# Issue order of one score chunk and of the router's steps in the attention stage of a diffusion layer

## What is computed

```python
fx, qx, kx, vx = split_projection(hx @ w_in[l])
qx = axial_rope(heads(qx, N_Q_HEADS, q_norm_g[l]), row, col)    # 12 heads of 64
kx = axial_rope(heads(kx, N_KV_HEADS, k_norm_g[l]), row, col)   # 4 heads of 64
...
s = jnp.einsum('bqkgd,bskd->bkgqs', qi, k_all).astype(jnp.float32) * (HEAD_DIM ** -0.5)
p = jax.nn.softmax(s, axis=-1).astype(v_all.dtype)              # over 1280 keys
o = jnp.einsum('bkgqs,bskd->bqkgd', p, v_all)
...
x = x + g1 * (jnp.concatenate([four_x, attn_x], axis=-1) @ w_out[l])
h = modulate(x, norm_ffn_g[l], sh2, sc2)
aff = jax.nn.softmax(jnp.einsum('bnd,de->bne', h, w_router), axis=-1)   # 16 experts
x = x + g2 * (the 16 experts on the 128 tokens that each of them picks by aff)
return rms_norm(x, final_norm_g)
```

## Time and profile before

| | |
|---|---|
| median of three runs | 2030.63 us (2030.01 to 2036.04) |
| the profiled execution: its own time | 2035.89 us |
| its span, first to last instruction | 2033.3 us |
| busy: TensorE, VectorE, ScalarE, GpSimd | 1856.9 us (91%), 1614.0 (79%), 1303.5 (64%), 290.0 (14%) |
| attention stage | about 266 to 862 us of the span |
| tile steps by the copy L921: 5th, 6th, 7th | 71.85, 71.88, 73.15 us |
| mean granted TensorE clock of the span | 0.964 of full speed |
| slot 1 of the step shown, scores to scores (619.85 to 623.17) | 3.32 us, TensorE without idle |
| TensorE, start to start: wide score chunk, then one item with its values (664.67, 665.23, 665.91) | 0.56 us, 0.68 us |

### The profile page before, as it was taken

How to read it: one execution, slowest core, us unless ns; L and a number is a source line. 1 busy time by engine, 2 the same in 40 slices (tenths; PEclk the granted TensorE clock), 3 DMA queues, 4 the chain that set the end, 5 groups by cost and what they waited for, 6 DMA issues and landing times.

```text
span 2033.3 us, 28027 instructions
## 1 busy us (share of the span) xinstructions
PE 1856.9 (91%) x8691; PEld 1462.4 (72%) x8691; DVE 1614.0 (79%) x2070; ACT 1303.5 (64%) x1921; POOL 290.0 (14%) x294
## 2 busy tenths in 40 slices
PE   6998869899899889719999999999999999999996
PEld 3776647666666666517888888888888888888884
DVE  5777547766766767487989998999899989998996
ACT  4444347666766766416777777777777777777774
POOL 0233221110111111101101100110011001110113
PEclk8999879999999999958999999999999999999998
DMA  8556480210110120039999999999999999999996
GB/s 353 172 151 170 109 228 28 63 41 22 62 44 28 52 62 10 31 120 365 396 394 390 376 377 402 389 381 370 405 386 384 368 404 386 373 384 398 380 379 245
DMA packets 108034, 512.28 MB, mean 252 GB/s; under 512 B 12064, under 2 KB 36040, under 8 KB 57296
## 3 DMA queue, kind: packets, MB, share of 16 engines
q1 hardware_dynamic: 101792, 489.11, 63.7%
q0 software_dynamic: 4752, 17.30, 3.2%
q10 hardware_dynamic: 1440, 5.24, 0.7%
HBM read 481.71 MB, written 27.28 MB: 250 GB/s over the span
## 4 chain that ended last, share of the span: by engine, by line
PE 54%; DVE 2%; DMA 1%; issue 0%; ACT 0%; POOL 0%
PE banks L1599 34%; PE banks L1624 17%; PE banks L1611 1%; PE banks L1580 1%; DVE topi L1458 1%; DVE top L1456 1%; DVE cand L1459 1%; DMA xe<-h_scratch,icol 0%; DVE raw L1554 0%; DMA out<-raw 0%; DVE ysc L1518 0%; DVE ysc L1561 0%; ACT d_hi L1421 0%; POOL out L1381 0%; DVE x_lo L1484 0%
## 5 line engine op out<-in xcount | busy, mean ns | idle before, releaser
L1490 DVE TENSOR_TENSOR w_lo<-raw,w_hi 128x2048 fp32r<-128x2048 f32 x256 | 574.8, 2287 | 67.9 <-ACT w_hi L1399 67.9
L1399 ACT ACTIVATE w_hi<-raw 128x2048 fp32r<-128x2048 f32 x256 | 470.8, 1919 | 10.5 <-DMA raw<-in_w_exp 10.4
L1599 PE MATMUL banks<-w_hi,x_hi 128*128 128x512 f32 x1024 | 406.2, 397 | 1.4 <-DVE x_lo L1484 1.4
L1599 PE MATMUL banks<-w_hi,x_lo 128*128 128x512 f32 x1024 | 400.6, 391 | 0.0
L1599 PE MATMUL banks<-w_lo,x_hi 128*128 128x512 f32 x1024 | 400.1, 391 | 0.0
L1498 DVE TENSOR_TENSOR d_lo<-raw,d_hi 128x1024 fp32r<-128x1024 f32 x256 | 296.2, 1218 | 1.5 <-ACT d_hi L1421 1.4
L1421 ACT ACTIVATE d_hi<-raw 128x1024 fp32r<-128x1024 f32 x256 | 258.1, 1060 | 38.5 <-DMA raw<-in_w_exp 24.7
L1058 DVE TENSOR_TENSOR ptl<-banks,pth 128x384 fp32r<-128x384 f32 x320 | 176.6, 555 | 66.8 <-ACT pth L995 61.5
L995 ACT ACTIVATE pth<-banks 128x384 fp32r<-128x384 f32 x320 | 156.9, 490 | 109.3 <-PE banks L1168 101.1
L1599 PEld LDWEIGHTS banks<-w_hi,x_lo 128*128 128x128 f32 x1024 | 192.9, 188 | 40.7
L1599 PEld LDWEIGHTS banks<-w_hi,x_hi 128*128 128x128 f32 x1024 | 193.2, 189 | 39.7 <-DVE x_lo L1484 1.8
(11 more groups left out here) (213 smaller groups left out, 2768.4 us busy)
## 6 DMA issues: line engine op xcount, KB each, us to landing
raw<-in_w_exp SPq DMA_DIRECT2D x384, 1024.0 KB, 8.0
a_ring<-in_w_mod SPq DMA_DIRECT2D x32, 512.0 KB, 5.0
qt<-q_scratch SPq DMA_DIRECT2D x64, 192.0 KB, 3.6
a_slot<-in_w_mod SPq DMA_DIRECT2D x8, 1024.0 KB, 12.0
a_w_raw<-in_w_in SPq DMA_DIRECT2D x3, 2048.0 KB, 30.2
q_scratch<-a_qst SPq DMA_DIRECT2D x16, 384.0 KB, 3.9
a_xt<-in_x ACTq DMA_DIRECT2D x8, 512.0 KB, 6.1
xr<-in_x SPq DMA_DIRECT2D x8, 512.0 KB, 4.0
```

Of the source, the lines that this page charges most:

```text
L1399: act.activation(w_hi[which][c][:, :], raw[which][c][:, :], ACT.Copy).then_inc(s["hi_done"], 1)
L1490: dve.tensor_tensor(w_lo[which][c][:, :], raw[which][c][:, :], w_hi[which][c][:, :].bitcast(F32), ALU.subtract).then_inc(s["lo_done"], 1)
L1599: i = pe.matmul(psum[:, 2 * (j % 2) + which, :], x_[par][:, k, :], w_, start=(k == 0 and w_ is hi and x_ is x_hi), stop=(k == KD - 1 and x ...
```

## The change

Four edits:

1. **Scores.** TensorE issues chunk 1 of a head at the end of part 1, behind that part's transposes and value products; chunk 2 follows at once at the start of part 2. VectorE reduces chunk 1 behind correction 1.
2. **Logit factor.** The first stage multiplies the key gain once by minus the logit factor. Scores then come out negated and scaled: VectorE takes minima (`mn`, in place of `mx` and `nb`), the small minimum is itself the bias, L1054 goes, and the exponential has scale -1.
3. **The shift of h2** is added on GpSimd in two halves of 512; HT0 waits for the first only, the store for both.
4. **Router chain.** HT0 stays at the end of slot 8 (part 3); HT1 moves from the end of slot 9 to its part 2, ahead of the fourth item; the router's product from the end of slot 10 to its part 0; maximum and negative to part 1 of slot 10; the exponential to part 2 of slot 10; reciprocal and scaling to part 0 of slot 11; the transpose to part 1 and the copy of the affinities to part 2 of slot 11.

```diff
@@ scaled (first stage, VectorE)
                 if n == 0:
                     dve.wait_ge(s["kv_tab"], 32)
+                    link(dve.tensor_scalar(g_qk[:, 1, :], g_qk[:, 1, :], -SCALE, None, ALU.mult))
@@ SP
-                    sp.wait_ge(s["h2b"], t if cur else t + 1)
+                    sp.wait_ge(s["h2b"], 2 * t)
@@ GpSimd
                     if prev and cur and i == 8:
                         pool.wait_ge(s["h2a"], t)
-                        pool.tensor_tensor(h2[:, :], h2[:, :], rows[:, SH2, :], ALU.add).then_inc(s["h2b"], 1)
+                        for c in (slice(0, 512), slice(512, D)):
+                            pool.tensor_tensor(h2[:, c], h2[:, c], rows[:, SH2, c], ALU.add).then_inc(s["h2b"], 1)
+                        pool.wait_ge(s["h2b"], 2 * t)
@@ ScalarE
                             act.activation(pr[(h // 3 % 2) * 3 + h % 3][:, lo:hi], psum[:, (NCH * h + c) % 4, 0:hi - lo], ACT.Exp,
-                                           bias=nb[:, h:h + 1], scale=SCALE, accum_out=den[:, h, c:c + 1]).then_inc(s["exp_done"], 1)
+                                           bias=mn[:, h, 3:4], scale=-1.0, accum_out=den[:, h, c:c + 1]).then_inc(s["exp_done"], 1)
...
+                        if prev and (i, c) == (9, 3):
...
+                        if prev and (i, c) == (10, 2):
+                            act.wait_ge(s["neg_done"], t)
...
+                        if prev and (i, c) == (11, 2):
+                            act.wait_ge(s["misc_mm"], misc(t, use["AF"]) + 1)
...
@@ VectorE
-                        if cur and c < NCH:
+                        if cur and c in (0, 2):
                             lo, hi = CH[c]
                             dve.wait_ge(s["s_done"], NS * t + NCH * i + c + 1)
-                            ins = dve.tensor_reduce(mx[:, i, c:c + 1], psum[:, (NCH * i + c) % 4, 0:hi - lo], AX, ALU.max)
+                            ins = dve.tensor_reduce(mn[:, i, c:c + 1], psum[:, (NCH * i + c) % 4, 0:hi - lo], AX, ALU.min)
                         if cur and c == NCH - 1:
                             chain(ins)
 
-                            chain(dve.tensor_reduce(mx[:, i, 3:4], mx[:, i, 0:3], AX, ALU.max))
-                            dve.tensor_scalar(nb[:, i:i + 1], mx[:, i, 3:4], -SCALE, None, ALU.mult).then_inc(s["nb_done"], 1)
+                            dve.tensor_reduce(mn[:, i, 3:4], mn[:, i, 0:3], AX, ALU.min).then_inc(s["mn_done"], 1)
                         if c < len(its):
...
+                        if cur and c == 1:
+                            lo, hi = CH[c]
+                            dve.wait_ge(s["s_done"], NS * t + NCH * i + c + 1)
+                            ins = dve.tensor_reduce(mn[:, i, c:c + 1], psum[:, (NCH * i + c) % 4, 0:hi - lo], AX, ALU.min)
...
+                        if prev and (i, c) == (10, 1):
+                            dve.wait_ge(s["misc_mm"], misc(t, use["RT"]) + 1)
+                            chain(dve.tensor_reduce(lg[:, 2, 1:2], psum[:, MB, 0:E], AX, ALU.max))
+                            dve.tensor_scalar(st2[:, 3:4], lg[:, 2, 1:2], -1.0, None, ALU.mult).then_inc(s["neg_done"], 1)
+                        if prev and (i, c) == (11, 0):
+                            dve.wait_ge(s["lexp"], t)
+                            chain(dve.reciprocal(lg[:, 2, 2:3], lg[:, 2, 0:1]))
+                            dve.tensor_scalar(lg[:, 0, :], lg[:, 1, :], lg[:, 2, 2:3], None, ALU.mult).then_inc(s["misc_free"], 1)
@@ TensorE (scores(i, c), turn(j) and route() hold the bodies of L1145 to L1153, L1202 to L1207 and L1209 to L1214)
-                        if cur and c < NCH:
+                        if cur and c in (0, 2):
+                            scores(i, c)
...
                             if kt >= 2:
                                 times(k - 2)
+                        if cur and c == 1:
+                            scores(i, c)
...
+                        if prev and (i, c) in ((8, 3), (9, 2)):
+                            turn(i - 8)
+                        if prev and (i, c) == (10, 0):
+                            route()
+                        if prev and (i, c) == (11, 1):
+                            misc_free("AF")
+                            pe.transpose(psum[0:E, MB, 0:P], lg[:, 0, :], ident[:, :]).then_inc(s["misc_mm"], 1)
```

More of the change, by code:

```diff
@@ L795, in nc_phase_b @@
     mix = sb("mix", [P, KD, P], F32, B)
[L796 to L797 removed]
+    mn = sb("mn", [P, NQ, 4], F32, B)
     den = sb("den", [P, NQ, 4], F32, B)
@@ L1016, in step @@
                         act.activation(junk2[:, :], x2[:, :], ACT.Square, accum_out=st2[:, 0:1]).then_inc(s["ss_done"], 1)
[L1017 to L1026, removed]
             schedule(step, act)
@@ L1139, in out_part, with scores, turn, route @@
                     return ins
+                def scores(i, c):
+                    lo, hi = CH[c]
+                    n = NCH * i + c
+                    if c == 0 and i % REP == 0:
+                        pe.wait_ge(q_in[i // REP], 32 * (t + 1))
+                    if not (isinstance(t, int) and t == 0 and n < 4):
+                        pe.wait_ge(s["exp_done"], NS * t + n - 3)
+                    o = psum[:, n % 4, 0:hi - lo]
+                    pe.matmul(o, qt[:, i, 0, :], ks[:, i // 3, lo:hi], start=True, stop=False)
+                    pe.matmul(o, qt[:, i, 1, :], ks[:, i // 3, lo:hi], start=False, stop=True).then_inc(s["s_done"], 1)
+                def turn(j):
+                    pe.wait_ge(s["h2b"], 2 * (t - 1) + 1 + j)
+                    if cur:
+                        misc_free(f"HT{j}")
+                    for k in range(4):
+                        ins = pe.transpose(psum[:, bank_of(f"HT{j}", cur), k * P:(k + 1) * P], h2[:, (4 * j + k) * P:(4 * j + k + 1) * P], ident[:, :])
+                    ins.then_inc(s["misc_mm"], 1)
+                def route():
+                    misc_free("RT" if cur else "HT1")
+                    for k in range(KD):
+                        if not cur and k == KD // 2:
+                            misc_free("RT")
+                        ins = pe.matmul(psum[:, MB, 0:E], h2t[:, k, :], wrt[:, k, :], start=(k == 0), stop=(k == KD - 1))
+                    ins.then_inc(s["misc_mm"], 1)
                 for i in range(NQ):
@@ L1143, in step @@
                     for c in range(NCH + 1):
-                        if cur and c < NCH:
-                            lo, hi = CH[c]
-                            n = NCH * i + c
-                            if c == 0 and i % REP == 0:
-                                pe.wait_ge(q_in[i // REP], 32 * (t + 1))
-                            if not (isinstance(t, int) and t == 0 and n < 4):
-                                pe.wait_ge(s["exp_done"], NS * t + n - 3)
-                            o = psum[:, n % 4, 0:hi - lo]
-                            pe.matmul(o, qt[:, i, 0, :], ks[:, i // 3, lo:hi], start=True, stop=False)
-                            pe.matmul(o, qt[:, i, 1, :], ks[:, i // 3, lo:hi], start=False, stop=True).then_inc(s["s_done"], 1)
+                        if cur and c in (0, 2):
+                            scores(i, c)
                         if c == 0 and i in fl:
@@ L1199, in step @@
                         out_part(i, EARLY, True, False)
-                    if prev and i in (8, 9):
-                        j = i - 8
-                        pe.wait_ge(s["h2b"], t if cur else t + j)
-                        if cur:
-                            misc_free(f"HT{j}")
-                        for k in range(4):
-                            ins = pe.transpose(psum[:, bank_of(f"HT{j}", cur), k * P:(k + 1) * P], h2[:, (4 * j + k) * P:(4 * j + k + 1) * P], ident[:, :])
-                        ins.then_inc(s["misc_mm"], 1)
-                    if prev and i == 10:
-                        misc_free("RT" if cur else "HT1")
-                        for k in range(KD):
-                            if not cur and k == KD // 2:
-                                misc_free("RT")
-                            ins = pe.matmul(psum[:, MB, 0:E], h2t[:, k, :], wrt[:, k, :], start=(k == 0), stop=(k == KD - 1))
-                        ins.then_inc(s["misc_mm"], 1)
-                    if prev and i == 11:
-                        misc_free("AF")
-                        pe.transpose(psum[0:E, MB, 0:P], lg[:, 0, :], ident[:, :]).then_inc(s["misc_mm"], 1)
             schedule(step, pe)
```

25 lines of the change are left out of this document (11 added, 14 removed).

## The result

The changed kernel takes 2020.35 us (median of 6 runs, 2018.65 to 2024.92), the kernel before, run beside it, 2032.04 us (2030.01 to 2036.04). The ratio is 0.9944, with an interval of 0.9934 to 0.9954: faster by 11.7 us, where 11.7 was forecast (2024.2 against 2035.89). The profiled execution took 2020.44 us, its span is 2018.5.

What follows compares the result with a forecast made beforehand. Outside the output projection, attention was taken as bound by waits across engines, not TensorE's pace. Seven tiles -9.7, first tile +1.0, clock -3.1, rest +0.1: -11.7 us on 2035.89 (2024.2), carried to 2019; range 2007 to 2031.

Steps and rivals of the forecast that it cites:

- The ring: Chain of dependent steps through the engines in a plain attention head: 3.74 us before, 3.93 forecast, 0.19 longer.
- After four items: Ring following a head with four items (0, 3, 6, 9), through correction 2: 4.30 us, 0.37 more than plain.
- The router's leg: From head 9's ones-matrix product to the next tile's at head 0, with router steps: -1.55 us from 17.40.
- The leg R6 to R9: Ones-matrix product at head 6 to that at head 9: -0.4 us from 15.42, shift halves removing 0.56 idle.
- R3 to R6: Ones-matrix product at head 3 to that at head 6, with output projection: unchanged at 26.00 us, bound +0.4.
- The first tile: Attention tile without router steps, so its last two legs only lose: 26.08 to 27.2 us, +1.0 in the sum.
- The clock: TensorE clock falls in two tiles, one seen behind the router's row-transpose wait, both taken away: -3.1 us.
- A: Rival, slower: in heads 8 to 11 VectorE's list takes the router's gain back; 2040 us; chance 0.10.
- B: Rival, much faster: the second minimum costs nothing and heads fall to TensorE's 3.3 us; 1999 us; chance 0.06.
- D: Rival: affinities copy keeps router steps on head 11's path, no gain at head 8; 2025.5 us; chance 0.14.
- C: Rival, no change: small idles remain and the clock falls once in each of seven tiles; 2029.6 us; chance 0.08.
- R0 to R3: Ones-matrix product at head 0 to that at head 3, without router steps: 13.05 to 13.62 us, +0.57.

Runs made afterwards that it cites:

- the old order: Changed kernel with the second score chunk and its minimum back at their old places, factor, shift halves and router moves kept: 2002.52 us.
- TensorE's half alone: Changed kernel with the second chunk kept behind the value products on TensorE, its minimum back ahead of correction 1 on VectorE: 2009.59 us.
- VectorE's half alone: Changed kernel with the second chunk back ahead of the transposes on TensorE, its minimum left behind correction 1 on VectorE: 2028.97 us.

## Why the prediction was right

**The ring.** The forecast was 3.93 us by eight intervals, and the trace shows 3.95 by the same eight. The experiments show the reason given for it: the slot gets longer since the second minimum stands behind correction 1, and slot 7 gets shorter by 0.58 (3.95 to 3.37) when only the minimum goes back. That is near the 0.60 that a 512-wide reduction takes until the next operation. The sum held the factor's gain of 0.19 as well: by itself the moved chunk costs 0.39 a plain slot (3.56 to 3.95), and the prediction never set it against the router's part on its own, which would have shown the headline of the change as a loss.

**After four items** I had 4.30; this is it in ScalarE's timeline, with the plain slot behind it:

```profile
612.72 0.69 ACT L981 ACTIVATE pr<-banks,mn 128x512 f32<-128x512 f32 x1
...
617.11 0.69 ACT L981 ACTIVATE pr<-banks,mn 128x512 f32<-128x512 f32 x1 [0.71 <-DVE mn L1055]
...
621.06 0.69 ACT L981 ACTIVATE pr<-banks,mn 128x512 f32<-128x512 f32 x1 [0.71 <-DVE mn L1055]
```

4.39, so 0.09 too little; with the 0.02 of the plain slot that is 0.11 of the 0.13 by which the leg missed (13.75 against 13.62).

**The router's leg** was the term most wrongly sized: -1.93 us where I had -1.55. Slot 10 came out as summed (5.30). For slot 11 I took 4.4 between 3.9 (all hidden) and 4.9 (the copy of the affinities holds the exponential); it measured 4.04. The copy had 0.31 us to spare, and the lower bound was nearer. The wait of the row transpose is below the 0.5 named.

**The leg R6 to R9** gave -0.57 (forecast -0.4): -0.78 from the halves, +0.21 from slot 7. The term mis-sized was the 0.56 of the halves. Half of the addition took 1.28 us (my estimate 1.2):

```profile
588.99 1.28 POOL L936 TENSOR_TENSOR h<-h,rows 128x512 f32<-128x512 f32 x1 [3.70 <-DVE h L1114]
```

R3 to R6 stood still (26.02 for 26.00).

**The first tile** lost 1.45 us in its last two legs (forecast 1.1), but gained 0.36 in the leg before them, so 1.1 in all.

**The clock** gave back 2.8 us (forecast 3.1). Granted clock over 520 us of the stage, kernel after (last columns: clock, DMA share, GB/s):

```profile
306.00:826.00 520.00, 480.77 (x2498) 343.78 (x2497) 362.82 (x810) 348.28 (x947) 81.13 (x97) 1.00 0.14 42
```

**The rivals.** A is out: the lists do not refill what the router's waits gave up, for the router's part gives 2.7 us a tile alone, against 0.7 needed. But its mechanism, VectorE's list, is what took 17.8 us of the gain; it lost only by the size of the rest. B is out by the plain slot of 3.95; a slot of TensorE's pace exists (3.37), but only with the minimum in its old place. D is out: the copy of the affinities holds nothing in slot 11, and the leg R6 to R9 has its gain. C is out: TensorE's small waits are still there (in the stage the score matmuls waited for ScalarE 38 times, 16.3 us in all, longest 0.8, and the transposes for VectorE's corrections 56 times, 16.0 us), and the clock did not fall once in seven tiles. The Trainium skill (TensorE: Matmul & The Clock Gate, "A second HAM failure mode: psum-queue depth-cycling") says of another kernel that frequent small idles between groups of matmuls made the clock swing. The trace of this kernel shows no such swing in its seven tiles. The time that the prediction gave for C was 2029.6 us, against 2020.35 measured.

**Median and profile.** The profiled execution of before lay above its median (2035.89; 2032.04 by all six runs), that of after on its own (2020.44, 2020.35). Carrying the forecast down by the full 5.3 us gave 2019, 1.4 below the median: the first three runs of before (median 2030.63) were a little fast. That 11.7 us were forecast and 11.7 measured is luck in its last figure. The sum was made for the profiled execution, and between the two profiled ones lie 15.4 us; between the mile posts 14.3 were gained where the same terms gave 11.8. The router's leg alone gave 2.7 us more over seven tiles than forecast, R6 to R9 some 1.2 more, and R0 to R3 0.9 less.

## What to carry to other kernels

When a wait is taken out of one engine's list, write down the whole ring through all engines, with start-to-start intervals, before and after: here TensorE lost a wait of 0.72 us, and the slot got 0.21 us longer, because the step that had filled another engine's pause (a minimum during ScalarE's copy) moved into the chain. Move the producer and its consumer one at a time; from the old order, the pair cost 17.8 us, TensorE's half alone 7.1, and VectorE's half alone 26.5: the halves do not add up, so neither could be read off the pair. A chain of small dependent steps is best spread so that each waits behind other work, and the last of them, the copy that stands ahead of the next head's exponential, decides how far it can be pushed.

## What the hardware showed that I had not expected

**The clock fell more often behind a longer wait.** In the kernels that leave the router's steps where they were, the router's row transpose has TensorE's longest wait of a tile. With the logit factor alone, TensorE's timeline shows

```profile
606.83 0.28 PE L1217 MATMUL banks<-ident,lg 128*16 128x128 f32 x1 [1.27 <-DVE lg L1110]
```

and the stretch of 5 us around it (last columns as above) keeps the full clock of 2.4 GHz:

```profile
606.00:611.00 5.00, 3.46 (x17) 2.46 (x17) 2.47 (x7) 3.09 (x9) 0.00 (x0) 1.00 0.62 184
```

With the moved chunk alone, the wait is longer, and the score matmul behind it has a row of 0.79 us where it has 0.50 in the earlier trace rows:

```profile
629.31 0.38 PE L1226 MATMUL banks<-ident,lg 128*16 128x128 f32 x1 [1.94 <-DVE lg L1114]
...
629.90 0.79 PE L1153 MATMUL banks<-ks,qt 128*128 128x512 f32 x1 [0.21 <-issue]
```

Its stretch of 5 us has the mean of the earlier trace rows, so part of it ran at 1.2 GHz:

```profile
629.00:634.00 5.00, 4.48 (x17) 3.49 (x17) 1.38 (x3) 2.45 (x7) 0.00 (x0) 0.66 0.51 155
```

Counted over the seven tiles with a router, one profiled execution of each kernel:

| wait ahead of the row transpose | kernel | tiles in which the clock fell |
|---|---|---|
| 0 to 0.27 us | after, and the nine others with the router's part | 0 of 7 in each |
| 1.27 us | factor alone | 0 of 7 |
| 1.46 us | before | 2 of 7 |
| 1.46 us | halves alone | 3 of 7 |
| 1.94 us | moved chunk alone | 7 of 7 |

So in these executions the factor's part, with 0.2 us less of wait, was without a fall as the router's part was, and the moved chunk, with 0.5 us more, had one in every tile. They are my reading of why that kernel came out at 2057 and not 2050; no run took them away by themselves. Between the tiles of one kernel with the same wait of 1.46 some lose the clock and some don't; what decides there stays open, as does whether the length of the wait alone decides, since the kernels differ in the work around it too.

**A row's idle is less than the gap.** Products that follow each other start 0.17 us apart while their rows last 0.34, so the idle that the trace shows ahead of a late one leaves some 0.17 us out. What the leg gained (0.78) is near the gap from start to start (0.73), not the 0.56 in the bracket that I had read off. What the kernel gains is another matter: with the halves alone 0.17 went again in the next leg, and a tile kept 0.57.
